# Turning tile 0 inside tile 1's sum and running two units by tiles behind it, in the second block of a two-block layer stack

## What the reference computes

```python
def second_block(x, ...):
    for l in range(DEPTH):                       # DEPTH = 2
        mix = mixer_sublayer(x, ..., w_in[l], ..., w_branch[l], w_out[l])
        x = layer_norm_2(ALPHA * x + mix, ln1_g[l], ln1_b[l])
        ff = jnp.square(jax.nn.relu(x @ w_ff1[l])) @ w_ff2[l]
        x = layer_norm_2(ALPHA * x + ff, ln2_g[l], ln2_b[l])
    return x
```

## Time and profile before

| what | value |
|---|---|
| runs | 1675.16, 1672.95, 1674.86 us; median 1674.86 |
| profiled execution: span of the core | 1675.87 us (no other time is given for it) |
| TensorE busy | 1635.3 us, 98% |
| VectorE / ScalarE / GpSimd busy | 890.5 / 721.8 / 32.6 us |
| mean granted TensorE clock | 0.991 |
| main memory traffic | 409.5 MB read, 245 GB/s over the span |

### The profile page before, as it was taken

The page is one execution under the profiler, slowest core; times in us unless marked ns, Lnnn a source line. Parts: engine busy times, 40 slices in busy tenths (PEclk is TensorE's granted clock), DMA queues, the critical chain, the costliest instruction groups (busy, mean ns, idle before and its releaser), DMA issues.

```text
span 1675.9 us, 25227 instructions
## 1 busy us (share of the span) xinstructions
PE 1635.3 (98%) x10724; PEld 1285.9 (77%) x10724; DVE 890.5 (53%) x1190; ACT 721.8 (43%) x1084; POOL 32.6 (2%) x56
## 2 busy tenths in 40 slices
PE   8999999998999999997999999999999999999998
PEld 7878644435988644434989998989989899988997
DVE  7777421104677411104658656655566676575555
ACT  4775211112675211113655544544456564444443
POOL 0000000000000000000000000000000000000000
PEclk9999999998999999998999999999999999999999
DMA  9637999997837999997745565555556455555552
GB/s 270 230 126 283 353 416 418 416 417 255 269 134 271 357 416 418 417 417 273 218 136 175 176 202 176 193 184 185 192 157 199 134 169 177 201 192 185 185 192 76
DMA packets 193109, 413.07 MB, mean 246 GB/s; under 512 B 16416, under 2 KB 130848, under 8 KB 176608
## 3 DMA queue, kind: packets, MB, share of 16 engines
q1 hardware_dynamic: 191904, 409.81, 68.3%
q10 hardware_dynamic: 1088, 1.57, 0.4%
HBM read 409.52 MB, written 1.84 MB: 245 GB/s over the span
## 4 chain that ended last, share of the span: by engine, by line
PE 90%; DVE 3%; DMA 3%; ACT 2%; issue 1%; SPq 1%; POOL 0%; ACTq 0%; DVEq 0%
PE PS L1700 13%; PE PS L513 11%; PE PS L517 11%; PE PS L514 11%; PE PS L521 9%; PE PS L525 9%; PE PS L524 9%; PE PS L1723 5%; DMA weights_raw<-in_w_in 3%; PE PS L540 2%; PE PS L1676 2%; PE PS L1732 2%; DVE hT_lo L729 1%; DVE weights_low L493 1%; ACT arena L863 0%
## 5 line engine op out<-in xcount | busy, mean ns | idle before, releaser
L493 DVE TENSOR_TENSOR weights_low<-weights_raw,weights_hi 128x1024 fp32r<-128x1024 f32 x368 | 431.2, 1216 | 199.7 <-ACT weights_hi L488 198.8
L488 ACT ACTIVATE weights_hi<-weights_raw 128x1024 fp32r<-128x1024 f32 x368 | 365.7, 1046 | 136.6 <-PE PS L525 66.6
L513 PE MATMUL PS<-hT_hi,weights_hi 128*128 128x256 f32 (+1 forms) x1456 | 411.4, 283 | 0.9 <-ACT bias L955 0.9
L517 PE MATMUL PS<-hT_hi,weights_low 128*128 128x256 f32 (+1 forms) x1456 | 409.6, 281 | 1.4 <-DVE weights_low L493 1.4
L514 PE MATMUL PS<-hT_lo,weights_hi 128*128 128x256 f32 (+1 forms) x1456 | 409.2, 281 | 0.0
L513 PEld LDWEIGHTS PS<-hT_hi,weights_hi 128*128 128x128 f32 (+1 forms) x1456 | 274.6, 189 | 4.8 <-issue 2.7
L517 PEld LDWEIGHTS PS<-hT_hi,weights_low 128*128 128x128 f32 (+1 forms) x1456 | 274.8, 189 | 2.0 <-DVE weights_low L493 1.8
L514 PEld LDWEIGHTS PS<-hT_lo,weights_hi 128*128 128x128 f32 (+1 forms) x1456 | 274.8, 189 | 1.2
L525 PE MATMUL PS<-weights_hi,opa_lo 128*128 128x512 f32 x384 | 152.6, 397 | 0.0
L521 PE MATMUL PS<-weights_hi,opa_hi 128*128 128x512 f32 x384 | 152.4, 397 | 0.2
L524 PE MATMUL PS<-weights_low,opa_hi 128*128 128x512 f32 x384 | 151.0, 393 | 0.0
(11 more groups left out here) (335 smaller groups left out, 2367.7 us busy)
## 6 DMA issues: line engine op xcount, KB each, us to landing
weights_raw<-in_w_in SPq DMA_DIRECT2D x80, 1024.0 KB, 5.5
weights_raw<-in_w_ff SPq DMA_DIRECT2D x64, 1024.0 KB, 5.2
arena<-in_w_down SPq DMA_DIRECT2D x22, 1024.0 KB, 22.8
arena<-in_w_gate SPq DMA_DIRECT2D x20, 1024.0 KB, 15.0
weights_raw<-in_w_up SPq DMA_DIRECT2D x20, 1024.0 KB, 17.3
weights_raw<-in_w_gate SPq DMA_DIRECT2D x20, 1024.0 KB, 17.6
arena<-in_w_up SPq DMA_DIRECT2D x16, 1024.0 KB, 13.7
weights_raw<-in_w_down SPq DMA_DIRECT2D x16, 1024.0 KB, 16.0
```

The costliest lines, as they stand in the source:

```text
L488: act.activation(u.flat[0][:, c:e], u.x[:, c:e], ACT.Copy).then_inc(*sig.mark("w_hi", u.u, i))
L493: dve.tensor_tensor(u.flat[1][:, c:e], u.x[:, c:e], u.flat[0][:, c:e].bitcast(F32), ALU.subtract).then_inc(*sig.mark("w_lo", u.u, i))
L513: pe.matmul(o, w[0], x[0], start=start, stop=False)
L517: return pe.matmul(o, w[1], x[0], start=False, stop=stop)
```

## The change

In the second block alone:

- The plan has ff1 0 and ff1 1 first, then ff1 i+2 and ff2 i in turn: ff1 is two stages ahead.
- The high places go from 3 to 4 (one of the three places that units of experts had), and the raw places from 5 to 7 (the other two). `feed` splits up to 4 units from the one fed.
- Tile 0 is turned inside tile 1's sum, before its last 6 matmuls (`late`), and VectorE writes tile 0's `hT_lo` before tile 1's sum (`turned_early`).
- `project_two_by_tiles` runs two units for tile 0, with tile 1 turned between the last two steps of the second, then both for tile 1. It replaces `project_tiles` and `keep_clock` for ff1 0 and ff1 1 of both layers and for gla v0 and gla v1 of layer 1.
- ff1 0 and ff1 1 both come with rows on partitions; both are copied by ScalarE and turned back inside ff1 2 (`turn_rows`).
- In ScalarE's and VectorE's loop stage i begins with feed(ff1 i+2) and ends with feed(ff2 i).

```diff
         cols("ff1 0", a["w_ff1_2"][l], 0)
+        cols("ff1 1", a["w_ff1_2"][l], 256)
         for i in range(16):
-            if i + 1 < 16:
-                cols(f"ff1 {i + 1}", a["w_ff1_2"][l], 256 * (i + 1))
+            if i + 2 < 16:
+                cols(f"ff1 {i + 2}", a["w_ff1_2"][l], 256 * (i + 2))
             rows(f"ff2 {i}", a["w_ff2_2"][l], 256 * i)
...
-        NRAW, NSPLIT, NOWN = 5, 3, 3
+        NRAW, NSPLIT, NOWN, MORE_SPLIT = 5, 3, 3, 4
...
+        own_hi = unrounded("own_at_hi", [P, NOWN, UNIT], dt=F32R)
...
+            ring = [NRAW + (second_block + i) % NSPLIT for i in range(NSPLIT)] + [AT_OWN[0]]
             for u, (name, *_) in enumerate(plan):
                 if not of_expert(name):
-                    at = min(range(NRAW), key=lambda i: free_from[i])
-                    d = dense % NSPLIT
-                    found.append((at, held[at], d, held[NRAW + d]))
+                    at = min((*range(NRAW), *(AT_OWN[1:] if dense >= second_block else ())), key=lambda i: free_from[i])
+                    split = NRAW + dense % NSPLIT if dense < second_block else ring[(dense - second_block) % MORE_SPLIT]
+                    found.append((at, held[at], split, held[split]))
...
-                    self.split_until(self.used + NSPLIT)
+                    self.split_until(self.used + (MORE_SPLIT if self.used >= second_block else NSPLIT))
...
                             for k in range(u.k):
+                                if late is not None and sp and t and half and k == 0:
+                                    late()
...
+        def project_two_by_tiles(pe, names, x, by, norm):
+            b = [banks.take(pe, name, by, among=4) for name in names]
+            for t in range(NT):
+                for i, name in enumerate(names):
+                    u = units[place[name]]
+                    if t == 0:
+                        use(pe, name)
+                    for k in range(KD):
+                        if t == 0 and i == 1 and k >= KD - 2:
+                            turn_half(pe, norm, 1, k - (KD - 2))
+                        if i == 0 and k % 4 == 0:
+                            pe.wait_ge(*sig.at("dve_took", f"{norm} T{t}{k // 4}"))
+                        last = rows_still(pe, PS[:, b[i], t * S:(t + 1) * S], u, at_k(x, k, t * P, (t + 1) * P),
+                                          at_k(u.pair, k, 0, S), k == 0, k == KD - 1, t == k == 0)
+                    if t == NT - 1:
+                        last.then_inc(*sig.mark("ps", name))
...
             for t in range(NT):
+                if t and turned_early:
+                    turned_lo(dve, label, 0)
                 dve.wait_ge(*sig.at("ps", f"{label} t{t}"))
...
             banks.turn = 0
-            project_tiles(pe, L("ff1 0"), hT, "act_took", among=4, norm=n_("ln1b"))
+            project_two_by_tiles(pe, L("ff1 0", "ff1 1"), hT, "act_took", n_("ln1b"))
+
+            def turn_rows():
+                for i in range(2):
+                    b = banks.take(pe, n_(f"ff1 {i} turned"), "act_took", among=4)
+                    pe.wait_ge(*sig.at("act_took", n_(f"ff1 {i}")))
+                    for t in range(NT):
+                        for c in range(2):
+                            last = transpose(pe, PS[:, b, c * S + t * P:c * S + (t + 1) * P], by_rows[i][:, t, c * P:(c + 1) * P])
+                    last.then_inc(*sig.mark("ps", n_(f"ff1 {i} turned")))
+                    yield
+
+            for i in range(N_STAGE - 2):
+                project_T(pe, L(f"ff1 {i + 2}"), hT, "act_took", among=4, between=turn_rows() if i == 0 else None)
+                pe.wait_ge(*sig.at("ff_dve", n_(f"up {i}")))
+                accumulate_rows(pe, L(f"ff2 {i}"), opa, 2 * (i % 4), n_("ln2b"), i == 0, False)
...
+            up_of = lambda i: n_(f"ff1 {i}" if i > 1 else f"ff1 {i} turned")
+            for i in range(2):
+                feed(n_(f"ff1 {i}"))
+                act.wait_ge(*sig.at("ps", n_(f"ff1 {i}")))
+                copy(by_rows[i], PS[:, banks.of(n_(f"ff1 {i}")), :].rearrange("p (t n) -> p t n", t=NT)).then_inc(
+                    *sig.mark("act_took", n_(f"ff1 {i}")))
+            for i in range(N_STAGE):
+                if i + 2 < N_STAGE:
+                    feed(n_(f"ff1 {i + 2}"))
+                act.wait_ge(*sig.at("ps", up_of(i)))
+                if i > 1:
+                    act.wait_ge(*sig.at("ff_dve", n_(f"up {i - 2}")))
+                act.activation(relu_t[i % 2], one_bank(banks.of(up_of(i)), 2), ACT.Relu).then_inc(
+                    *sig.mark("act_took", up_of(i)))
+                act.wait_ge(*sig.at("ff_dve", n_(f"square {i}")))
+                if i > 3:
+                    act.wait_ge(*sig.at("ps", n_(f"ff2 {i - 4}")))
+                q = 2 * (i % 4)
+                hi_part(act, opa[0][:, q:q + 2, :], relu2[i % 2]).then_inc(*sig.mark("ff_act", n_(f"up {i}")))
+                if i < N_STAGE - 2:
+                    feed(n_(f"ff2 {i}"))
```

More of the change, by code:

```diff
@@ L423, in assign_places, with dense_before @@
             return found
-        before_experts = [sum(not of_expert(p[0]) for p in plan[:place[f"ple gate 3 {l}"] + 1]) for l in range(DEPTH)] + [len(plan)]
+        def dense_before(u):
+            return sum(not of_expert(p[0]) for p in plan[:u])
+        before_experts = [dense_before(place[f"ple gate 3 {l}"] + 1) for l in range(DEPTH)] + [len(plan)]
+        second_block = dense_before(place["gla v0 0"])
         unit_place = assign_places()
@@ L436, in __init__ @@
                 if not self.expert:
[L437 removed]
+                    hi = own_hi[:, d - AT_OWN[0], 0:size] if d in AT_OWN else w_hi[:, d - NRAW, 0:size]
+                    low = own_hi[:, self.raw - AT_OWN[0], 0:size] if self.raw in AT_OWN else low_in_place[:, self.raw, 0:size]
+                    self.flat = hi, low
                     self.pair = tuple(v.rearrange("p (k n) -> p k n", k=self.k) for v in self.flat)
@@ L604, in project_rows, with accumulate_rows @@
             sig.also("ps", f"{label} t1")
-        def accumulate_rows(pe, names, x, k_of, label, first, final, ready=(), turns=False, midway=None):
+        def accumulate_rows(pe, names, x, k_of, label, first, final, ready=(), turns=False, midway=None, late=None):
             groups = [(n,) for n in names[:-2]] + [names[-2:]] if turns else [(n,) for n in names]
@@ L767, in norm_vector @@
                     dve.wait_ge(*sig.at("params_in", label))
-                elif turned:
+                elif turned and not turned_early:
                     turned_lo(dve, label, 0)
@@ L2140, in tensor_block2 @@
             n_ = lambda name: f"{name} {l}"
-            project_tiles(pe, L("gla v0"), hT, "act_took", among=4, norm="ln2 1" if l == 0 else "ln2b 0")
-            project_tiles(pe, L("gla v1"), hT, "act_took")
+            if l == 0:
+                project_tiles(pe, L("gla v0"), hT, "act_took", among=4, norm="ln2 1")
+                project_tiles(pe, L("gla v1"), hT, "act_took")
+            else:
+                project_two_by_tiles(pe, L("gla v0", "gla v1"), hT, "act_took", "ln2b 0")
             project_T(pe, L("gla q0", "gla q1"), hT, "act_took")
@@ L2251, in tensor_block2 @@
                 pe.wait_ge(*sig.at("merge_dve", n_(f"split {i}")))
-                accumulate_rows(pe, L(f"w_out {2 * i}", f"w_out {2 * i + 1}"), opa, 4 * i, n_("ln1b"), i == 0, i == 1, turns=i == 1)
+                accumulate_rows(pe, L(f"w_out {2 * i}", f"w_out {2 * i + 1}"), opa, 4 * i, n_("ln1b"), i == 0, i == 1, turns=i == 1,
+                                late=(lambda: turn_tile(pe, n_("ln1b"), 0)) if i == 1 else None)
             banks.turn = 0
-            project_tiles(pe, L("ff1 0"), hT, "act_took", among=4, norm=n_("ln1b"))
@@ L2256, in turn_first @@
-            def turn_first():
-                b = banks.take(pe, n_("ff1 0 turned"), "act_took", among=4)
-                pe.wait_ge(*sig.at("act_took", n_("ff1 0")))
-                for t in range(NT):
-                    for c in range(2):
-                        last = transpose(pe, PS[:, b, c * S + t * P:c * S + (t + 1) * P], relu_t[1][:, t, c * P:(c + 1) * P])
-                last.then_inc(*sig.mark("ps", n_("ff1 0 turned")))
-                yield
-            for i in range(N_STAGE):
-                if i + 1 < N_STAGE:
-                    project_T(pe, L(f"ff1 {i + 1}"), hT, "act_took", among=4, between=turn_first() if i == 0 else None)
-                if i < N_STAGE - 2:
-                    pe.wait_ge(*sig.at("ff_dve", n_(f"up {i}")))
-                    accumulate_rows(pe, L(f"ff2 {i}"), opa, 2 * (i % 4), n_("ln2b"), i == 0, False)
+            project_two_by_tiles(pe, L("ff1 0", "ff1 1"), hT, "act_took", n_("ln1b"))
@@ L2389, in scalar_block2 @@
             feed(n_("w_out 3"))
-            up_of = lambda i: n_(f"ff1 {i}" if i else "ff1 0 turned")
-            for i in range(N_STAGE + 1):
-                if i < N_STAGE:
-                    feed(n_(f"ff1 {i}"))
-                    if i == 0:
```

(16 more changed lines are left out.)

53 lines of the change are left out of this document (29 added, 24 removed).

## The result

| | median of the runs | lowest and highest | runs |
|---|---|---|---|
| before | 1674.89 us | 1672.95 to 1676.91 | 7 |
| after | 1679.12 us | 1678.04 to 1681.19 | 7 |

The ratio is 1.0026, with a 95% interval of 1.0016 to 1.0036: the changed kernel is 4.2 us slower. The forecast was 1681.8 in a range of 1675.2 to 1686.5, so the direction was right, the time lies in the range, and the loss came out at 4.2 us and not at 6.95. The profiled execution of after has a span of 1678.0 us (its run took 1679.21) and a mean granted clock of 0.994.

What follows compares the result with a forecast made beforehand. TensorE, busy 98% of the span, was taken to bound the kernel. Gains of -5.55 us, stages +5.0, bank +5.9 and clock +1.6 made +6.95 us, forecasting 1681.8 us against the median 1674.86, range 1675.2 to 1686.5.

Steps and rivals of the forecast that it cites:

- Handovers: After ln2b and ln1b: turning inside the sum and two units by tiles gain 2.15, 1.55 and 1.3 us.
- the 0.27 that I had held back for layer 1: Tile 0 turned inside the sum: 0.27 us more allowed in layer 1.
- two waits inside the sum: Last sum units: two gaps of TensorE before the transposes, near 0.4 and 0.25 us.
- The bank: Stage 2: ff1 4 waits for relu 2 to read bank 2, 2.95 us once a layer, 5.9 us in all.
- rivals 1 and 2: Feed-forward loop: neither bank nor stages stall (9%), 1669.3 us; only the stages stall (6%), 1674.7 us.
- The clock: Behind stage 2's wait: half clock costs 0 to 1.6 us per layer; one drop counted, 1.6 us.
- The stages: Stages 1 and 3 to 13: up i comes late for ff2 i, 0.21 us a stage, 5.0 us in all.
- Rival 3: Feed-forward loop: the bank stalls, the stages do not; 1675.2 to 1678.4 us, chance 10%.
- Raw places: Second block's loads: seven raw places let SyncE load two units further ahead; costed at nothing.
- rival 4: Handovers: the clock falls at each, three times 1.6 us on top of the forecast, 1686.6 us; chance 5%.
- The rule weighed in the prediction: Handovers: transposes do not count as busy for the clock like matmuls, so it could drop at each; sum +11.8 us.

Runs made afterwards that it cites:

- e6: e2 with tile 0 turned behind the sum instead of inside it, its low part behind tile 1's sum; 1670.61 us, ratio 0.9972 to before.
- e1: The changed kernel with the bank turn set to 3 behind stage 1, so ff1 4 takes bank 3; 1671.6 us, ratio 0.9976 to before.
- e2: The changed kernel with feed(ff1 i+2) moved behind up i on ScalarE and VectorE; 1667.86 us, ratio 0.9950 to before.
- e3: e2, but stage 2 alone feeds ff1 i+2 first, as in the changed kernel; 1675.43 us, ratio 0.9999 to before.
- e4: The changed kernel with matmuls of no use just before ff1 4, 20 a layer; 1677.39 us, ratio 1.0013 to before.
- e5: The changed kernel with five raw places in the second block instead of seven; 1682.25 us, ratio 1.0043 to before.
- e8: e2 run once more, unchanged; 1665.25 us, ratio 0.9941 to before.
- e9: e2 with the ring of four high places reordered, own_at_hi second instead of last; 1668.1 us, ratio 0.9954 to before.

## Why the prediction was right, and where it was off

**Handovers: right.** The sum ends at E + 1.56 (forecast 1.61) and both units are through at E + 14.46 (14.4); each gain is 0.14 to 0.35 larger than forecast: ff1 2 with both turnings back took 1059.58 - 1053.06 = 6.52 and not 6.67, and the 0.27 that I had held back for layer 1 was not lost. e6 shows that the half with the turning inside the sum carries 0.88 a handover. I had expected two waits inside the sum, near 0.4 and 0.25; there are two, 0.41 before the first half and some 0.2 before the second, of which only the first shows as a bracket (0.25).

**The bank: right, in place and size.** 2.99 us a layer against 2.95, at ff1 4 and nowhere else, released by relu 2. e1 removes it by the bank alone, e2 by the place of the feed alone, and e3 brings it back alone. That closes rivals 1 and 2, in which it would not stand.

**The clock: right in number, not understood.** One drop of two, 1.58 us. That it would be one of two was a guess that came out, not something I had worked out. e4 fits an idle time that brings it down, no more. Why layer 1 and not layer 0 stays open: the same wait of 2.73 did it in layer 1 of after, e3 and e5, and in layer 0 of none.

**The stages: the one term that was mis-sized.** I wrote 12 x 2 x 0.21 = 5.0, and by the lengths it came to 2.7. The stall itself is what I had worked out: 0.20, as e1 and e2 differ by it. It stands in stage 1 too. The timeline of VectorE and TensorE of after, layer 0:

```profile
1070.13 0.69 DVE L761 TENSOR_TENSOR opa_lo<-arena,opa_hi 128x512 fp32r<-128x512 f32 x1 [0.70 <-ACT opa_hi L758]
1070.88 0.50 PE L530 MATMUL PS<-weights_hi,opa_hi 128*128 128x512 f32 x1
1071.22 0.39 PE L533 MATMUL PS<-own_at_hi,opa_hi 128*128 128x512 f32 x1
```

The low part ends at 1070.82, ff2 1 starts 0.06 later and its next matmul 0.34 behind that, as in the other stages. That stage 1 is only 11.30 and 11.27 long, start to start, and 0.2 shorter over both layers than before, has other reasons: most of its stall falls behind ff2 1's start, and before's stage 1 began with a late ff2 0.

What was missing is that matmuls do not have one pace. By taking high and raw places from the experts' units, the change moved every other ff2 unit to places from which it runs 0.6 to 1.7% faster than the 0.233 of before, and ff1's products differ by unit too (5.64 us for the ff1 at 1156.04 in e2, where the earlier trace rows have 5.70). e2, in which nothing stalls, is 0.062 us a stage shorter than before over the 22 stages 3 to 13 of both layers, 1.4 us; after is 0.194 us a stage longer there than e2, 4.3 us; and 4.3 - 1.4 is the 2.9 of the table. The 0.8 us of the two stretches outside the stages are in no term of my sum either. I had taken the spacing of one row of before, 0.233, for a constant of the shape. Rival 3, no stall in the stages, would have come nearer to the time (1675.2 to 1678.4) but for a wrong reason.

**Raw places: the right number for this change, with a wrong reason.** I costed them at nothing because no wait of before goes back to a load, and named a lead of several units as the cover. Since the change has all seven, nothing was lost; but e5 shows that with five the same order loses 883.70 - 878.56 = 5.1 us in length. What was missing in my argument: a new order of units makes new due times for loads, and the absence of a wait in the old order says nothing of them.

**The clock in the handovers: rival 4 is out.** The window over the handover has 1.00 with 16 transposes in it and no kept clock. The rule weighed in the prediction (the Trainium skill, TensorE: Matmul & The Clock Gate, Part 4) could have had it fall; in these runs, with products between the turnings, it did not.

What stays open: why layer 0 keeps its clock, and why the memory place of the weights changes the pace. For ff1 it is the other way round: in e2 the spacing of its units is 0.1189 to 0.1200 with the low part in own_at_hi and 0.1173 to 0.1186 with it in weights_low. It was 0.1186 in every ff1 unit of before, so the name of the place does not settle it alone.

## What to carry to other kernels

An engine that works in order makes a split fed ahead into a wait for everything that stands behind it: before a stage runs further ahead, ask which unit frees the place that the first instruction of the loop fills, and put that instruction behind the work that is due sooner. The move cost two blocks of a few lines and made of a loss of 0.26% a gain of 0.5 to 0.6%: e2 beats both kernels. Count banks and places by hand through the first stages of a loop, since one rotation that comes out wrong in a single stage can cost as much as a change of the whole order gains.

## What the runs showed of the hardware that I had not expected

- The spacing of 128x512 matmuls at the full clock was 0.229 to 0.2335 us by where in memory the high and low weights lay, repeated within 0.001 over three kernels (e2, e8, e9).
- With nothing changed in their instructions, two stretches of some 240 us were 0.45 and 0.37 shorter in after than in before, and with five raw places instead of seven (e5) the difference was gone to within 0.05.
- The same idle time of 2.73 us amid dense work brought the clock to the 1.2 GHz level in layer 1 and not in layer 0, in one execution each of three kernels (after, e3, e5); with 20 matmuls in the wait, and 0.50 idle, it stayed full in both (e4).
